# Placing the first pair of an RWKV scan from the operand stage, waiting for its last stores inside the scan, and taking two chained norms as one root

## The reference, cut to what matters

```python
def step(S, inp):                      # rwkv7_scan, one token
    r_t, w_t, k_t, v_t, a_t, b_t = inp
    sa = jnp.einsum('bhvk,bhk->bhv', S, a_t)
    S = S * w_t[:, :, None, :] + sa[..., None] * b_t[:, :, None, :] + v_t[..., None] * k_t[:, :, None, :]
    y = jnp.einsum('bhvk,bhk->bhv', S, r_t)
    return S, y
```

## Time and profile before

| | us |
|---|---|
| median of 3 runs (4195.14 to 4206.39) | 4202.31 |
| the profiled execution | 4202.03 |
| its span, first to last instruction | 4200.2 |
| operand part's last DVE operation ends | 1711.6 |
| first matmul of the scan | 1725.3 |
| first product behind the tail's roots | 3249.6 |

### The profile page before, as it was taken

One profiled execution on the slowest core, in us unless ns is written; L12 is line 12 of the kernel. 1 busy time (PEld: TensorE's weight loads), 2 busy tenths in 40 slices (PEclk: granted clock), 3 DMA queues, 4 the chain that ended last, 5 costly groups with the idle time before them and its releaser, 6 DMA issues. The chain is left out here.

```text
span 4200.2 us, 67202 instructions
## 1 busy us (share of the span) xinstructions
PE 3834.1 (91%) x30328; PEld 3127.3 (74%) x30328; DVE 1960.7 (47%) x1966; ACT 1255.5 (30%) x1341; POOL 914.8 (22%) x488
## 2 busy tenths in 40 slices
PE   8999999999989999577777999999997999997797
PEld 6778888888767776476674888888876888875675
DVE  5554221222444128444445445444446888837432
ACT  5552211111334448222225311111134222112412
POOL 1142422223222111223221223232322000000221
PEclk9999999999999999799998999999998999997898
DMA  2111111111111336411103111111111322223332
GB/s 90 45 48 45 62 54 51 39 47 55 35 52 56 111 99 202 145 64 59 50 28 115 56 42 59 57 61 54 62 59 45 110 78 75 79 76 93 130 106 95
DMA packets 145021, 303.62 MB, mean 72 GB/s; under 512 B 14097, under 2 KB 77585, under 8 KB 142417
## 3 DMA queue, kind: packets, MB, share of 16 engines
q1 hardware_dynamic: 127648, 263.15, 19.6%
q10 hardware_dynamic: 17088, 36.18, 2.2%
HBM read 233.75 MB, written 65.54 MB: 71 GB/s over the span
## 5 line engine op out<-in xcount | busy, mean ns | idle before, releaser
L2557 DVE SCALAR_TENSOR_TENSOR H<-hy_cu,par,H 128x1024 f32<-128x1024 f32 x120 | 153.2, 1277 | 0.0
L2557 DVE SCALAR_TENSOR_TENSOR hy_odd<-hy_cu,par,hy_odd 128x1024 f32<-128x1024 f32 x112 | 143.1, 1277 | 0.0
L219 POOL TENSOR_TENSOR wlo0A<-wraw0A,whi0A 128x1024 fp32r<-128x1024 f32 (+3 forms) x30 | 65.5, 2185 | 291.4 <-ACT whi0A L210 291.3
L479 POOL TENSOR_TENSOR flow_hl<-flow_up,flow_hh 128x1024 fp32r<-128x1024 f32 x44 | 106.5, 2420 | 94.5 <-ACT flow_hh L447 94.5
L2963 POOL MEMSET ssm_toep<- 128x4096 f32 x1 | 3.5, 3511 | 551.0 <-POOLq L2660 551.0
L1828 POOL TENSOR_TENSOR sc_NT<-sc_Gx,sc_level 128x512 f32<-128x512 f32 x80 | 100.2, 1271 | 98.8 <-PE psA L1606 78.3
L939 DVE SCALAR_TENSOR_TENSOR tm_t<-tm_xn,par,tm_t 128x1024 f32<-128x1024 f32 x24 | 35.4, 1484 | 174.4 <-ACT tm_t L799 174.4
L219 POOL TENSOR_TENSOR wlo0B<-wraw0A,whi0B 128x1024 fp32r<-128x1024 f32 (+2 forms) x29 | 60.8, 2095 | 252.9 <-ACT whi0B L210 252.8
L502 DVE TENSOR_TENSOR flow_up<-flow_up,flow_gate 128x1024 f32<-128x1024 f32 x44 | 112.6, 2560 | 6.3 <-ACT flow_gate L439 1.9
L219 POOL TENSOR_TENSOR wlo0C<-wraw0A,whi0C 128x1024 fp32r<-128x1024 f32 (+3 forms) x29 | 61.7, 2127 | 182.2 <-ACT whi0C L210 182.2
L219 POOL TENSOR_TENSOR wlo0A<-wraw0B,whi0A 128x1024 fp32r<-128x1024 f32 (+3 forms) x29 | 52.9, 1825 | 217.6 <-ACT whi0A L210 217.6
(11 more groups left out here) (1290 smaller groups left out, 11498.2 us busy)
## 6 DMA issues: line engine op xcount, KB each, us to landing
sc_ops<-rw_arbkv SPq DMA_DIRECT2D x16, 1280.0 KB, 6.2
wraw1A<-hybrid_in_dram SPq DMA_DIRECT2D x24, 512.0 KB, 3.5
wraw1B<-hybrid_in_dram SPq DMA_DIRECT2D x24, 512.0 KB, 3.5
wraw0A<-ffn_in_dram SPq DMA_DIRECT2D x22, 512.0 KB, 3.4
wraw0B<-ffn_in_dram SPq DMA_DIRECT2D x22, 512.0 KB, 3.4
wraw1A<-ffn_in_dram SPq DMA_DIRECT2D x22, 512.0 KB, 3.4
wraw1B<-ffn_in_dram SPq DMA_DIRECT2D x22, 512.0 KB, 3.3
wraw0A<-rkv_dram SPq DMA_DIRECT2D x16, 512.0 KB, 4.0
```

The costliest lines, as they stand in the source:

```text
L219: pl.tensor_tensor(wlo[n % 3][:, 0:kt, :], wraw[n % 2][:, 0:kt * P].rearrange("p (k n) -> p k n", n=P), whi[n % 3][:, 0:kt, :].bitcast(fp3 ...
L479: pl.tensor_tensor(hl[:, i, :], up, hh[:, i, :].bitcast(fp32), ALU.subtract)\
L2557: op = dve.scalar_tensor_tensor(out=acc, in0=c[:, j:j + T], scalar=w, in1=acc, op0=ALU.mult, op1=ALU.add)
```

## The change

1. The scan's `ops` and constants get their places (SBUF tiles) already in the first layer, in room that the operand part no longer reads at its end. SP, after `load_v(7)`, loads into it pair 0 of QD: tiles 0 to 5 whole, of tiles 6 and 7 the v part, and the four constants (six DMAs, awaited at the end of the block). ACT copies the first 128 tokens of ks, aa, rr and ab of tiles 6 and 7 from SBUF (eight copies). In the scan, `score` of chunks 0 and 1 waits for no load.
2. The wait for the ten last stores is no longer SP's at the end of the block; SP, ACT, POOL and DVE each have it at the start of their scan programs (`stored_before`). PE has none.
3. SP's program of the scan becomes: rt of pair 0, then for each further pair its two halves and its rt.
4. The second norm is folded: r12 = 1/sqrt(mean((g^2 + eps) h^2) + eps^2). ACT's first square has the scale weight = sqrt(g^2 + eps), made at the start of the second layer's block by two DVE operations and an ACT Sqrt on 128 x 8. r12 needs one Ln and one Exp; r1 has its Ln and Exp behind the eight high parts of x12, and DVE waits for it before `x(0)`.

```diff
@@ TimeMixIn.emit, SP @@
                         store(m - 2)
                         load_v(m)
+                    ops, smask, slevel, sfirst, seye = scan_first
+                    sp.wait_ge(*after("w_mm", at["k", DT - 1] + 1))
+                    for name in ("ks", "aa", "rr", "ab"):
+                        for m in (DT - 4, DT - 3):
+                            sp.wait_ge(*op_free(name, m + 2))
+                    sp.dma_start(ops[:, 0:DT - 2, :, :].rearrange("p m j t -> p (m j t)"),
+                                 QD[0, :, 0:DT - 2, :, :].rearrange("p m j t -> p (m j t)")).then_inc(*tick("ops_first", 16))
+                    sp.dma_start(ops[:, DT - 2:DT, 4, :], QD[0, :, DT - 2:DT, 4, :]).then_inc(*tick("ops_first", 16))
+                    for t, name in ((smask, "scan_mask"), (slevel, "scan_level"), (sfirst, "scan_first")):
+                        sp.dma_start(t[:, :, :], A[name]).then_inc(*tick("ops_first", 16))
+                    sp.dma_start(seye[:, :], A["scan_ident"]).then_inc(*tick("ops_first", 16))
                     store(DT - 2)
                     store(DT - 1)
-                    for name in ("rr", "ks", "aa", "ab", "vv"):
-                        for z in range(2):
-                            sp.wait_ge(*op_free(name, DT + z))
+                    sp.wait_ge(*after("ops_first", 96))
@@ TimeMixIn.emit, ACT @@
+                    for m in (DT - 2, DT - 1):
+                        for i, (name, j) in enumerate((("ks", 0), ("aa", 2), ("rr", 1), ("ab", 3))):
+                            act.wait_ge(*after("op_q", 4 * m + i + 1))
+                            act.activation(scan_first[0][:, m, j, :], L[name](m % 2)[:, 0:2 * CHUNK], ACT.Copy).then_inc(*tick("ops_last"))
@@ rwkv_scan @@
+                def stored_before(eng):
+                    for n in ("rr", "ks", "aa", "ab", "vv"):
+                        for z in range(2):
+                            eng.wait_ge(*after(f"op_out_{n}_{z}", 0))
...
-                        for t, name in ((smask, "scan_mask"), (slevel, "scan_level"), (sfirst, "scan_first")):
-                            sp.dma_start(t[:, :, :], A[name]).then_inc(*tick("sc_const", 16))
-                        sp.dma_start(seye[:, :], A["scan_ident"]).then_inc(*tick("sc_const", 16))
+                        stored_before(sp)
+
                         def load(p):
                             for h in range(2):
-                                if p >= 1:
-                                    sp.wait_ge(*(after("pe_time", 4 * p) if h == 0 else after("pe_W", order(2 * p - 1, 0) + 1)))
+                                sp.wait_ge(*(after("pe_time", 4 * p) if h == 0 else after("pe_W", order(2 * p - 1, 0) + 1)))
...
                             if p >= 1:
                                 sp.wait_ge(*after("pe_y", 2 * p))
                             sp.dma_start(rt[:, :, :], QD[p, :, :, RTS, :]).then_inc(*tick("rt_in", 16))
-                        load(0)
-                        for p in range(PAIRS):
-                            if p + 1 < PAIRS:
-                                load(p + 1)
+                        load_rt(0)
+                        for p in range(1, PAIRS):
+                            load(p)
                             load_rt(p)
...
-                                pe.wait_ge(*after(f"ops_in_{h}", 16 * (n // 2 + 1)))
+                                if n >= 2:
+                                    pe.wait_ge(*after(f"ops_in_{h}", 16 * (n // 2)))
@@ Tail @@
+            def emit(self, block):
+                @block.vector
+                def _(dve):
+                    g = par[:, COL["norm_final"]:COL["norm_final"] + DT]
+                    dve.tensor_tensor(self.weight, g, g, ALU.mult).then_inc(*tick("tail_g2"))
+                    dve.wait_ge(*after("tail_g2", 1))
+                    dve.tensor_scalar(self.weight, self.weight, RMS_EPS, None, ALU.add).then_inc(*tick("tail_g2"))
+                @block.scalar
+                def _(act):
+                    act.wait_ge(*after("tail_g2", 2))
+                    act.activation(self.weight, self.weight, ACT.Sqrt).then_inc(*tick("tail_weight"))
...
+            def scalar_root(self, act, z):
+                total, root, turn = self.sums[z], self.squares[z], self.turns[z]
+                act.wait_ge(*after("tail_mean", z + 1))
+                act.activation(total, self.W.flat(turn), ACT.Ln, bias=eps[:, 4:5] if z == 0 else eps[:, 0:1]).then_inc(*self.W.out(turn))
+                act.wait_ge(*self.W.freed(turn))
+                act.activation(root, total, ACT.Exp, scale=-0.5).then_inc(*tick("tail_r"))
@@ HybridIn.emit, ACT and DVE @@
-                    tail.scalar_root(act)
+                    tail.scalar_root(act, 0)
                     act.wait_ge(*after("w_mm", last_read + 1))
                     for m in range(DT):
                         act.wait_ge(*after("x12", m + 1))
                         act.activation(xh[:, m, :], tmp[m % 2], ACT.Copy).then_inc(*tick("x12_hi"))
+                    tail.scalar_root(act, 1)
...
-                    tail.vector_root(dve)
                     dve.wait_ge(*after("gain", 1))
-                    dve.wait_ge(*after("tail_r", 2))
+                    dve.wait_ge(*after("tail_r", 1))
...
                     dve.memset(cu[:, :, 0:LEAD], 0.0).then_inc(*tick("cu_lead"))
+                    dve.wait_ge(*after("tail_r", 2))
                     for m in range(DT // 2):
                         x(m)
```

More of the change, by code:

```diff
@@ L1068, in first_layer @@
                 weight_ring(c)
+                with ExitStack() as c1:
+                    scan_first.append(sb("sc_ops", [P, DT, 5, 2 * CHUNK], fp32, c1))
+                    for name, n in (("mask", 2), ("level", 5), ("first", 2), ("eye", 1)):
+                        scan_first.append(sb(f"sc_{name}", [P, n, CHUNK] if n > 1 else [P, CHUNK], fp32, c1))
                 xh, xl = (sb(f"flow0_{n}", [P, DT, T], r32, c) for n in ("xh", "xl"))
@@ L1832, in ready @@
                             pl.wait_ge(*gone(("bx", n)))
-                        pl.wait_ge(*after("sc_const", 64))
+                        stored_before(pl)
                         for p in range(PAIRS):
@@ L1908, in y_out @@
                                .then_inc(*out(("yu", n)))
+                        stored_before(dve)
                         dve.memset(S[:, 0, :, :], 0.0).then_inc(*tick("sc_S"))
-                        dve.wait_ge(*after("sc_const", 64))
                         for n in range(2):
@@ L2127, in scalar @@
                     if z == 0:
+                        act.activation(dst, H[:, m, :], ACT.Square, scale=self.weight[:, m:m + 1]).then_inc(*tick("tail_sq"))
+                    else:
                         act.activation(dst, H[:, m, :], ACT.Square).then_inc(*tick("tail_sq"))
-                    else:
-                        act.activation(dst, H[:, m, :], ACT.Square, scale=pcol("norm_final", m)).then_inc(*tick("tail_sq"))
             def vector(self, dve, m):
@@ L2147, in tensor @@
                     mm.then_inc(*tick("tail_mean"))
[L2149 to L2163, removed]
-                tb = self.turns[1]
-                dve.wait_ge(*after("tail_e", 1))
-                dve.wait_ge(*after("tail_mean", 2))
-                dve.tensor_tensor(b, self.W.flat(tb), sa, ALU.mult).then_inc(*self.W.out(tb))
-                dve.wait_ge(*after("tail_l", 1))
-                dve.tensor_tensor(b, a, sb_, ALU.add).then_inc(*tick("tail_both"))
+            def scalar_root(self, act, z):
[4 more added lines that the diff above has]
+                act.activation(root, total, ACT.Exp, scale=-0.5).then_inc(*tick("tail_r"))
             def passed(self):
-                passed({"tail_sq": 2 * DT, "tail_sum": 2 * DT - 2, "tail_mean": 2, "tail_e": 1, "tail_l": 1, "tail_r": 2, "tail_both": 1})
+                passed({"tail_sq": 2 * DT, "tail_sum": 2 * DT - 2, "tail_mean": 2, "tail_r": 2, "tail_g2": 2, "tail_weight": 1})
         BT_ = dram("ssm_btd", [SU, P, 2 * 4 * P])
@@ L2488, in emit @@
                 xs = [(xh[:, k, :], xl[:, k, :]) for k in range(DT)]
-                r1, r12 = tail.squares
+                r12, r1 = tail.squares
                 dst = {"zc": ZC, "u": U_, "zs": ZS, "gc": GC, "gs": GS}
@@ L2660, in second_layer @@
                 with nc.Block() as block:
+                    tail.emit(block)
                     O.emit(block, X)
```

32 lines of the change are left out of this document (18 added, 14 removed).

## The result

The changed kernel takes **4218.38 us** (median of 15 runs, 4210.9 to 4233.86) against 4202.31 of before: ratio **1.0037 [1.0028, 1.0046]**, 16.1 us slower. The profiled execution has a span of 4223.9 us, and it was 5.1 us late before it came to the change (at PE's matmul of 1690 us; SP's load of v at 1698.05 was at 1692.69 in the earlier trace rows); the profiles of the experiments stand between 1.8 us early and 4.6 us late at that matmul. So shifts are read against the stretch before them.

What follows compares the result with a forecast made beforehand. It took PE's 28.6 us wait at the scan's start, instruction pauses in the scan and an ACT/DVE chain in the tail as bounds. Sum: 4202.0 - 7.8 - 5.7 + 46.8 = 4235.3 us; range 4219 to 4250.

Steps and rivals of the forecast that it cites:

- Part 1: Scan's start: first pair loaded early, PE's scores hidden under the last stores; gain 7.8 us (bounds 6 and 10.9).
- Part 2: Waits for the last stores inside the scan: only DVE's is on the path, already counted in the scan start's gain.
- Part 3: Scan's load order: loads 2 to 7 queue behind rt's wait; loss 7.8 us a pair, 46.8 us in all.
- So a stall of any length earns one block: Scan stalls: PE gains one fetched block of 256 instructions per stall, saving one pause, taken as 1.6 us.
- the forecast's own test: Scan: forecast wrong if ops loads went before rt's wait ended, or PE ran twice 256 instructions more without a pause.
- Load(1) is spared: Scan's first pairs: load(1) isn't delayed, since rt(0) waits for nothing of the scan; loads 2 to 7 are hit.
- Part 4: Tail's root: fewer operations and table loads before the first x12; gain 5.7 us, with nothing lost behind it.
- The late loads cost more: Scan rival: the loads' burst meets PE's instruction fetch, adding 10 us, 4245; chance 0.15.
- The late loads are free: Scan rival: fetching runs on through stalls, pauses pay the 9.4 us, leaving 4188.5; chance 0.05.
- the prefetch brings nothing at the scan's start: Scan start rival: last store delayed by as much as saved, or ops_first holds the block; 4243, chance 0.08.
- half-way case: Scan: two or three pauses saved and SP's loads quicker, ending near 4205; chance 0.05, left out of the range.
- the main case: Whole kernel: the summed forecast of 4235, chance 0.67, with bounds 4209 and 4250.

Runs made afterwards that it cites:

- the eight profiles of the old order: Profiles of the kernel before and of seven experiment kernels, all running the scan's loads in the same order as the kernel before.
- order_only: The kernel before with the new order of SP's scan loads alone: 4240.5 us, ratio 1.0093.
- half_ahead: The changed kernel with half 0 of the next pair issued ahead of rt's wait, half 1 behind it: 4202.17 us, ratio 1.0009.
- prefetch_only: The kernel before with first pair and masks placed early and stores waited for inside the scan, old load order and tail: 4190.93 us, ratio 0.9975.
- twice_loaded: The kernel before with each operand load of pairs 1 to 7 issued again into a spare tile nothing reads: 4214.48 us, ratio 1.0053.

## Why the forecast was right in sign and off in size

- **Part 1, right.** 7.8 forecast, 7.9 to 8.1 in the trace of the kernel after, 10.5 (6.3 to 14.7) as a time of its own. The last store lands 2.7 to 3.0 us later, 3.1 worked out. Wrong in detail: "PE does both halves of score(0) between 1713 and 1717.5". It starts at 1720.09, about 1715 in the time of before, because stores take up to 2.33 us to issue behind the prefetches. It was covered all the same.
- **Part 2, right as far as the trace shows.** One wait on the path, DVE's memset; no run takes this part by itself.
- **Part 3, right in mechanism and place, mis-sized in what a stall gives back; this is the step that failed.** "So a stall of any length earns one block", worth 1.6 us, is the sentence. In the 300 matmuls behind each of the six places, PE's pauses are 2.6 us on average in the eight profiles of the old order (2.1 to 3.0) and 0.1 to 0.2 in after, order_only and half_ahead: the two pauses behind the stall go, not one. After the stall at 1889.64 PE came through some 990 matmuls and weight loads, with pauses of only 0.41 and 0.28 us and the 1.1 us for half 1, before one of 1.8. So the forecast's own test, "if PE ran twice 256 instructions more without a pause", went against it.
- **The account of a stall.** Between 1814 and 2190, against the mean of the eight, after and order_only have 48.7 us of waits for the loads and 18 us less in pauses for instructions, and run 12.7 us longer between the waits, at a granted clock of 0.91 and 0.92 against 0.95 to 1.00. By stall that is 8.1 + 2.1 - 3.0 = 7.2 us. The forecast had 9.4 - 1.6 = 7.8. Its "half 0 lands at T + 7.6, half 1 at T + 10.65" was T + 9.0 and T + 12.1, and x_both(2) begins 10.4 us later than before, not 9.4. The two errors go opposite ways, so 43 us for the six being near 46.8 is partly luck. Whether the two pauses go because blocks were fetched during the stall, or because PE runs slower behind it and its next block comes in time, no run separates.
- **Missing from Part 3: the first two pairs.** "Load(1) is spared" is right, but load(2) going late also spares PE long pauses there: 8.6 us gained from 1732 to 1814 against 4.0 in the old order, so 4.6 more. With the stalls, 43.4 - 4.6 = 38.8, where order_only measured 39.1 (32.3 to 45.4) and the forecast had 46.8.
- The Trainium skill (Runtime: NRT & Kernel Launch, Instruction fetch mechanics) was weighed in the forecast's Part 3, with its two sizes for the fetched part. The trace lies between what they would make of it: far from free, and more than one block recovered, two pauses of 2.6 us in all.
- **Part 4, right at the roots** (5.3 to 5.8 of 5.7 over the seven profiles with the new tail; 7.1, between 2.9 and 10.9, as a time). What is late next is as said: from 3262 to 3420 PE has one wait in the kernel after, 5.8 us for the first low part, and none behind it.
- **Missing from the sum: the place of the hidden tiles**, 6.3 us. The forecast priced the instructions of the new tail and never its tile. This and the load order are the two terms that took 4235 below the range: 6.3 + 7.7, with 2.7 and 1.4 from the other two, which lie within their intervals.
- **The rivals.** "The late loads cost more" named something real, since traffic does lengthen pauses; but in the late order the traffic falls where PE stands anyway, which was the argument against it. "The late loads are free" is excluded by order_only, and "the prefetch brings nothing at the scan's start" by prefetch_only.
- **The range** was too narrow at its low end. It left out a half-way case at 4205, with two or three pauses saved; two were, and the truth lay between that and the main case.

## What to carry to other kernels

A load that stands ahead of an unrelated wait on its queue is free and behind it is not: order the loads of a queue by when they can go, before anything is gained elsewhere; here that order alone turned 20 us won into 16 lost. A stall of an engine that is also short of instructions costs less than its delay, but not nothing: here 7.2 us of the 10.2 that waiting and the lower clock behind it took. And a new tile, however small, moves the ones behind it: before crediting a gain or a loss to code, add the tile without the code.

## What the runs showed of the hardware

- The matmuls of 128x512 that read one tile started 0.2333 us apart at its old place, 0.2290 at 32 bytes further, and 0.2333 again on average at 64 bytes further: 6.3 us of kernel (2.5 to 10.1) for an unused tile. In the first layer the same move gave nothing. Why is open.
- Operand traffic that no engine waits for cost 22 us in twice_loaded, while the fetches of PE's instructions went on beside it; about half of what its profile loses in the scan is longer waits of PE.
- Behind a stall of 7 us PE read 0.50 for 6.3 us (1889.7 to 1896.0 of the kernel after). Six such stalls brought the scan's granted clock from 0.95 to 1.00 down to 0.91 and cost 12.7 us of slower running, against 18 us of pauses that PE no longer made.
- Over the profiles, the same scan varies by 10 us between 1814 and 2190 (370.1 to 380.3) and by 10 between 1732 and 1814 (73.4 to 83.6). One profile does not price a term of that size; the medians of the kernels with one part each did.
